# Moving tiles in the on-chip memory by 32 or 64 bytes, in a float32 transformer kernel

## The chip, the cores and the metric

The kernel runs on one core of a Trainium2 chip. The metric is the time of one launch in microseconds (us) of device time; lower is better. TensorE does the matrix products, VectorE (DVE) and ScalarE (ACT) the elementwise work, GpSimd (POOL) a little of it, and SyncE (SP) issues nearly all DMA transfers from device memory.

## What is computed

Two transformer blocks in float32 on 256 tokens of width 2048, batch 1. The first block is a pooling mixer layer (project 2048 to 2 x 4096, causal mean pools in four groups of 1024 channels, a 1024 x 1024 product in each group, a gate, project back) and a multi-head attention layer with latent keys and queries (16 heads, chunk-causal). The second block has a modulation vector `silu(c) @ w_mod` (2048 x 12288), an attention layer with 16 sliding-window heads and 16 top-k selected heads, and a gated feed-forward layer of inner width 5632 with a 3-tap convolution. Cut to what matters, all the heavy products have this form:

```python
h = rms_norm(x, norm_ffn) * (1.0 + sc2) + sh2
u, g = jnp.split(h @ w_up, 2, axis=-1)            # 2048 x 11264
u = conv3(u) + conv_b
x = x + g2 * ((jax.nn.silu(u) * g) @ w_down)      # 5632 x 2048
```

Each weight is used once, for all 256 tokens. About 480 MB are read, nearly all of it weights.

## The kernel before

**A slab.** All weights come as a stream of slabs, 128 partitions x 1024 float32 (4096 bytes in each partition), as a rule two k-tiles of 128 rows by 512 columns. A slab goes through a ring of four slots, `s = 0..3`. SP loads it into `raw[s]`. ACT copies it, rounded to the float32r type that TensorE takes at full rate, to `w_hi[s]` (line 611). DVE writes what the rounding left out, `raw - w_hi`, to `w_lo[s]` (line 1063). The activations are split in the same way into a high and a low tile of 1024 bytes per k-tile: `h_hi`/`h_lo`, `pool_hi`/`pool_lo`, `y_hi`/`y_lo`, `hk_hi`/`hk_lo`, `f_hi`/`f_lo` and a few more.

**A product.** `gemm` (the function around the line that the profile gives as L1690) takes for every slab 24 matrix instructions: for each of four column tiles of 128 weights and each of the two k-tiles, weights `w_hi` against the high and the low activations (16 instructions), then weights `w_lo` against the high activations (8). In each the 128 x 128 weight tile is the stationary operand (LDWEIGHTS, named PEld in the profile) and 256 tokens of the activation are the moving one (MATMUL). The weights of the next instruction are loaded while the present one streams. `acc<-h_hi,w_hi` in a row means: moving `h_hi`, stationary `w_hi`.

**Order.** TensorE's order is written out by hand; ACT and DVE count slabs (`split_to`) and put their other work between two splits. SP waits only for a slot to come free. Modulation tiles (`mod_raw`, `mod_acc`, line 1051) are worked off at due times between slabs. Outside `gemm` TensorE does the small attention products, column sums with a tile `ones`, and transposes.

**Homes.** Every tile has a fixed byte offset in its partition. `home(start, end)` hands out offsets one behind the other, rounded up to 32 bytes. The constants on line 121 give the regions: LOW (x, raw, tmp, tables), MOD_AT, W_AT (the eight weight slots), MID (tiles of a stage, reused from stage to stage), H_AT (h_hi, h_lo), FAR (further tiles of a stage) and the three modulation slots at the end. Slots and activation tiles are multiples of 1024 bytes long, so that every k-tile and every column tile of one buffer starts at the same residue of 128 bytes. Residues of the start offsets, worked out from these lines:

| tiles | offset before | mod 128 |
|---|---|---|
| raw0..3 | 32896 + 4096 s | 0 |
| w_hi0..3 | 82048 + 4096 s | 0 |
| w_lo0..3 | 98432 + 4096 s | 0 |
| h_hi, h_lo | 148288, 164672 | 64 |
| pool_hi/lo and hk_hi, y_hi/lo, f_hi/lo, c and q | 181056 and on | 64 |
| y_mid_hi, y_mid_lo (the y tiles of the third group) | 127616, 135808 | 0 |
| hk_lo | 114816 | 0 |
| mod_acc, prob | 73824, 220128 and on | 96 |
| m_prob, table | 139392, 57472 | 0 |

Of the kernel before, what the change touches and what calls it, by code (L numbers as in the profile page):

```python
# [16 lines left out]
F32R = mybir.dt.float32r  # L17
# [5 lines left out]
P = 128  # L23
TOK = 256
# [36 lines left out]
RING = 4  # L61
# [3 lines left out]
SLAB = SLAB_K * SLAB_N  # L65
# [52 lines left out]


SB_END = 229344  # L120
LOW, MOD_AT, W_AT, MID, H_AT, FAR = 16512, 73824, 82048, 114816, 148288, 181056
MOD_RING = 3
MOD_RAW_AT = SB_END - MOD_RING * 4096

# [56 lines left out]
def two_block_kernel(nc, t, out, cols):  # L181

    fixed = ExitStack()
    with fixed:
        def home(start, end):

            at = [start]

            def sb(name, shape, dt=F32):
                tile = nc.alloc_sbuf_tensor_at(name, shape, dt, offset=at[0])  # L190
                at[0] += -(-4 * int(np.prod(shape[1:])) // 32) * 32
                assert at[0] <= end, (name, at[0], end)
                return tile

            return sb
# [27 lines left out]
        warm = low("warm", [P, 1])  # L223

        mod_acc = home(MOD_AT, W_AT)("mod_acc", [P, D])
        ring = home(W_AT, MID)
        w_hi = [ring(f"w_hi{s}", [P, SLAB], F32R) for s in range(RING)]
        w_lo = [ring(f"w_lo{s}", [P, SLAB], F32R) for s in range(RING)]
        h_sb = home(H_AT, FAR)
        h_hi = h_sb("h_hi", [P, KD, TOK], F32R)  # L230
        h_lo = h_sb("h_lo", [P, KD, TOK], F32R)
# [25 lines left out]
        mid, far = home(MID, H_AT), home(FAR, MOD_RAW_AT - 1024)  # L257
        pool_hi = far("pool_hi", [P, 8, TOK], F32R)
        pool_lo = far("pool_lo", [P, 8, TOK], F32R)
        y_hi = far("y_hi", [P, 8, TOK], F32R)  # L260
        y_lo = far("y_lo", [P, 8, TOK], F32R)
        gate_a = mid("gate_a", [P, 8, TOK])
# [34 lines left out]
        far = home(FAR + 16384, MOD_RAW_AT - 1024)  # L297
# [12 lines left out]
        far = home(FAR, MOD_RAW_AT)  # L310
# [22 lines left out]
        mid, far = home(MID, H_AT), home(FAR, SB_END)  # L333
# [2 lines left out]
        f_raw = mid("f_raw", [P, 4, TOK])  # L336
        y_tok = [mid(f"y_tok{m}", [P, HALVES, 512]) for m in range(4)]
        x_gained = [conv, conv_silu, f_raw, mid("x_gained3", [P, 4, TOK])]
        f_hi = [far(f"f_hi{s}", [P, 4, TOK], F32R) for s in range(2)]
        f_lo = [far(f"f_lo{s}", [P, 4, TOK], F32R) for s in range(2)]  # L340


        raw_landed = [sem(f"raw_landed{s}") for s in range(RING)]
# [1857 lines left out]
```

How the kernel before makes its waits and increments, by code:

```python
            def load_mod():  # L407
                while mod_loads.total() < MOD_RING or mod_loads.total() < min(6 * MOD_TILES, MOD_RING + mod_due(slabs.total() - RING - 1)):
                    n = mod_loads.total()
                    v, j, slot = n // MOD_TILES, n % MOD_TILES, n % MOD_RING
                    if n >= MOD_RING:
                        sp.wait_ge(mod_used, n + 1 - MOD_RING)
                    sp.dma_start(mod_raw[slot][:, :], t["w_mod_2"][0][(j // 2) * P:(j // 2 + 1) * P, bass.ds(v * D + (j % 2) * 1024, 1024)])\
                        .then_inc(mod_landed[slot], 16)
                    mod_loads.step()
# [1 line left out]
            def load(src, k, n):  # L418
                sp.wait_ge(lo_ready, slabs.value(1))
                s = slabs.slot(RING)
                sp.dma_start(raw[s][:, 0:k * n].rearrange("p (k n) -> p k n", k=k),
                             src.rearrange("(k p) n -> p k n", p=P)).then_inc(raw_landed[s], 16)
                slabs.step()
                n = slabs.total()
                if n >= 2 * RING:
                    load_mod()
                if n == LINES_AT:
                    sp.wait_ge(line_ready, 1)
                    sp.dma_start(line_rows[:, :], lines[:, :]).then_inc(lines_out, 16)
                if 0 <= n - BIAS_STORE_AT < 2 * HEADS:
                    bias_store(n - BIAS_STORE_AT)
                if 0 <= n - BIAS_LOAD_AT < HEADS:
                    bias_load(0, n - BIAS_LOAD_AT)
```

## Time and profile before

| | |
|---|---|
| runs | 2190.24, 2191.16, 2227.77 us; median 2191.16 |
| span of the profiled execution | 2196.8 us |
| PE / PEld busy | 2107.0 (96%) / 2066.5 (94%) us |
| DVE / ACT busy | 1580.5 (72%) / 1007.4 (46%) us |
| DMA | 481.13 MB, 219 GB/s mean |
| granted TensorE clock, mean | 0.975 |

The span goes from the first to the last instruction of one profiled execution; no other time of that execution is given. The span stands 5.6 us above the median of the runs. A busy PE only says that some matrix instruction was in flight: they overlap, one is in flight for about 280 ns while a new one starts every 113 to 120 ns. The distance from start to start, the spacing, is what counts, and it is read from how many instructions fall in a window.

### The profile page before, as it was taken

How to read it: one execution, taken by the hardware profiler on the slowest of the kernel's cores; microseconds unless marked ns; L12 is line 12 of the kernel's file. 1: busy time of each engine (PE TensorE's matmuls, PEld its weight loads, DVE VectorE, ACT ScalarE, POOL GpSimd, SP SyncE). 2: the span in 40 equal slices, each digit the busy share in tenths (PEclk: the TensorE clock that was granted, in tenths of full speed). 3: DMA queues.
4: the chain of work that ended last, by engine and by line, in shares of the span. 5: the costliest groups of instructions: out<-in, count | busy, mean ns of one | idle time of the engine just before them, and what ended most of it. 6: DMA issues, size and time to landing. Idle time of an engine off the chain costs nothing.

```text
span 2196.8 us, 41578 instructions
## 1 busy us (share of the span) xinstructions
PE 2107.0 (96%) x17878; PEld 2066.5 (94%) x17878; DVE 1580.5 (72%) x2040; ACT 1007.4 (46%) x1285; POOL 42.1 (2%) x87
## 2 busy tenths in 40 slices
PE   7999999999999999999899778889999999999998
PEld 7999999999999999999899667789999999999997
DVE  7998796697687877787776567666666666666665
ACT  5443443444455665654444453544444444444443
POOL 1000000000000000000000110100000000000000
PEclk9999999999999999999999898999999999999998
DMA  7897887889575786668698244246666666666663
GB/s 241 275 338 270 299 299 255 270 293 326 197 244 170 243 267 227 201 238 314 210 339 269 50 123 147 87 135 191 198 196 193 193 193 193 190 202 192 193 194 103
DMA packets 248430, 481.13 MB, mean 219 GB/s; under 512 B 28331, under 2 KB 57623, under 8 KB 248247
## 3 DMA queue, kind: packets, MB, share of 16 engines
q1 hardware_dynamic: 247487, 478.26, 67.2%
q8 instruction: 141, 2.31, 0.4%
q14 instruction: 42, 0.34, 0.0%
q0 software_dynamic: 528, 0.15, 0.0%
q10 hardware_dynamic: 232, 0.06, 0.0%
HBM read 476.27 MB, written 8.44 MB: 221 GB/s over the span
## 4 chain that ended last, share of the span: by engine, by line
PE 86%; DVE 7%; issue 2%; DMA 2%; ACT 2%; POOL 0%; SPq 0%; DVEq 0%; ACTq 0%
PE acc L1690 81%; PE side L1690 2%; PE sums L1690 2%; DMA mod_raw<-in_w_mod 1%; DVE w_lo L1063 1%; DVE mod_acc L1051 1%; ACT w_hi L611 1%; POOL prob L591 0%; DMA vec_rows<-in_conv_b 0%; PE side L1919 0%; DVE prob L1523 0%; DVE prob L1521 0%; DVE a_max L1402 0%; DVE probT L1564 0%; PE sums L1919 0%
## 5 line engine op out<-in xcount | busy, mean ns | idle before, releaser
L1063 DVE TENSOR_TENSOR w_lo<-raw,w_hi 128x1024 fp32r<-128x1024 f32 x679 | 829.8, 1229 | 487.1 <-ACT w_hi L611 486.3
L611 ACT ACTIVATE w_hi<-raw 128x1024 fp32r<-128x1024 f32 x679 | 717.4, 1060 | 938.3 <-PE acc L1690 845.7
L1690 PE MATMUL acc<-h_hi,w_hi 128*128 128x256 f32 x3728 | 890.4, 280 | 17.4 <-issue 14.1
L1690 PE MATMUL acc<-h_lo,w_hi 128*128 128x256 f32 x3728 | 885.5, 279 | 0.0
L1690 PEld LDWEIGHTS acc<-h_hi,w_hi 128*128 128x128 f32 x3728 | 707.6, 190 | 23.8 <-issue 19.0
L1690 PEld LDWEIGHTS acc<-h_lo,w_hi 128*128 128x128 f32 x3728 | 708.2, 190 | 0.3 <-issue 0.2
L1690 PE MATMUL acc<-h_hi,w_lo 128*128 128x256 f32 x3728 | 507.1, 279 | 0.0
L1690 PEld LDWEIGHTS acc<-h_hi,w_lo 128*128 128x128 f32 x3728 | 465.3, 190 | 0.0
L1051 DVE SCALAR_TENSOR_TENSOR mod_acc<-mod_raw,silu_c,mod_acc 128x1024 f32<-128x1024 f32 x180 | 230.4, 1280 | 14.1 <-DMA mod_raw<-in_w_mod 13.9
L1690 PE MATMUL acc<-f_hi,w_hi 128*128 128x256 f32 x704 | 164.9, 277 | 4.0 <-DVE xT L1176 4.0
L1690 PE MATMUL acc<-f_lo,w_hi 128*128 128x256 f32 x704 | 164.8, 277 | 0.0
L1690 PEld LDWEIGHTS acc<-f_hi,w_hi 128*128 128x128 f32 x704 | 132.7, 189 | 4.2 <-DVE xT L1176 4.2
L1690 PEld LDWEIGHTS acc<-f_lo,w_hi 128*128 128x128 f32 x704 | 132.8, 189 | 0.0
L1690 PE MATMUL acc<-f_hi,w_lo 128*128 128x256 f32 x704 | 94.8, 277 | 0.0
L1690 PE MATMUL acc<-y_hi,w_hi 128*128 128x256 f32 x384 | 94.4, 285 | 0.0
L1690 PE MATMUL acc<-y_lo,w_hi 128*128 128x256 f32 x384 | 92.0, 279 | 0.0
L1176 DVE SCALAR_TENSOR_TENSOR xT<-acc,mod,xT 128x256 f32<-128x256 f32 x208 | 86.0, 476 | 4.6 <-PE acc L1690 4.6
L1690 PEld LDWEIGHTS acc<-f_hi,w_lo 128*128 128x128 f32 x704 | 87.2, 189 | 0.0
L1690 PEld LDWEIGHTS acc<-y_hi,w_hi 128*128 128x128 f32 x384 | 73.4, 191 | 0.2 <-DVE tmp L1206 0.2
L1690 PEld LDWEIGHTS acc<-y_lo,w_hi 128*128 128x128 f32 x384 | 73.2, 191 | 0.0
L1690 PE MATMUL acc<-pool_hi,w_hi 128*128 128x256 f32 x256 | 59.6, 276 | 0.0
L1690 PE MATMUL acc<-pool_lo,w_hi 128*128 128x256 f32 x256 | 59.6, 276 | 0.0
(312 smaller groups left out, 2048.5 us busy)
## 6 DMA issues: line engine op xcount, KB each, us to landing
mod_raw<-in_w_mod SPq DMA_DIRECT2D x192, 512.0 KB, 6.0
raw<-in_w_up SPq DMA_DIRECT2D x176, 512.0 KB, 4.4
raw<-in_a_w_in SPq DMA_DIRECT2D x128, 512.0 KB, 5.1
raw<-in_w_down SPq DMA_DIRECT2D x88, 512.0 KB, 4.3
raw<-in_a_w_out SPq DMA_DIRECT2D x64, 512.0 KB, 4.7
raw<-in_w_in SPq DMA_DIRECT2D x56, 512.0 KB, 4.3
raw<-in_b_w_in SPq DMA_DIRECT2D x40, 512.0 KB, 4.6
raw<-in_a_w_group SPq DMA_DIRECT2D x32, 512.0 KB, 5.4
```

The costliest lines, as they stand in the source:

```text
L611: last = act.activation(w_hi[s][:, :], raw[s][:, :], ACT.Copy)
L1051: ins = dve.scalar_tensor_tensor(o, x[:, :], silu_c[:, j // 2:j // 2 + 1], o, ALU.mult, ALU.add)
L1063: last = dve.tensor_tensor(w_lo[s][:, :], raw[s][:, :], f32(w_hi[s][:, :]), ALU.subtract)
L1176: last = dve.scalar_tensor_tensor(x, acc[s][:, n, :], mod[:, scale, bass.ds(m + n, 1)], x, ALU.mult, ALU.add)
L1690: return pe.matmul(o, lhsT, rhs, start=start, stop=stop, skip_group_check=True)
```

## The change

The offsets of tiles change and nothing else: no instruction, no order, no wait, no size.

```diff
-LOW, MOD_AT, W_AT, MID, H_AT, FAR = 16512, 73824, 82048, 114816, 148288, 181056
+LOW, MOD_AT, W_AT, MID, H_AT, FAR = 16512, 73824, 82048, 115136, 148288, 181088
...
-        ring = home(W_AT, MID)
-        w_hi = [ring(f"w_hi{s}", [P, SLAB], F32R) for s in range(RING)]
-        w_lo = [ring(f"w_lo{s}", [P, SLAB], F32R) for s in range(RING)]
+        w_hi = [home(W_AT + 4128 * s, MID)(f"w_hi{s}", [P, SLAB], F32R) for s in range(RING)]
+        w_lo = [home(W_AT + 16512 + 4128 * s, MID)(f"w_lo{s}", [P, SLAB], F32R) for s in range(RING)]
...
         pool_lo = far("pool_lo", [P, 8, TOK], F32R)
+        far = home(FAR + 16384 + 64, MOD_RAW_AT - 1024)
         y_hi = far("y_hi", [P, 8, TOK], F32R)
         y_lo = far("y_lo", [P, 8, TOK], F32R)
...
-        f_hi = [far(f"f_hi{s}", [P, 4, TOK], F32R) for s in range(2)]
-        f_lo = [far(f"f_lo{s}", [P, 4, TOK], F32R) for s in range(2)]
+        f_sb = [home(FAR + 8256 * s, SB_END) for s in range(2)]
+        f_hi = [f_sb[s](f"f_hi{s}", [P, 4, TOK], F32R) for s in range(2)]
+        f_lo = [f_sb[s](f"f_lo{s}", [P, 4, TOK], F32R) for s in range(2)]
```

The residues of 128 bytes that follow: w_hi and w_lo of slot s at 32 s (0, 32, 64, 96); h_hi and h_lo at 64, as before; pool, hk_hi, c and q at 96; y_hi and y_lo at 32; f_hi and f_lo at 96 (buffer 0) and 32 (buffer 1); everything in MID, y_mid and hk_lo with it, at 64. The raw slots, x, tmp and the modulation tiles stay.

## Rows read from the trace of the kernel before

**Rows 1.** The page: busy time of the engines, and two rows of the span's 40 slices.
```profile
PE 2107.0 (96%) x17878; PEld 2066.5 (94%) x17878; DVE 1580.5 (72%) x2040; ACT 1007.4 (46%) x1285; POOL 42.1 (2%) x87
...
PEclk9999999999999999999999898999999999999998
```
**Rows 2.** The chain that ended last, by engine, and its longest pieces (start, us, what).
```profile
PE 86%; DVE 7%; issue 2%; DMA 2%; ACT 2%; POOL 0%; SPq 0%; DVEq 0%; ACTq 0%
...
1454.90 709.67 PE acc L1690 x6240
```
**Rows 3.** The page, costliest groups: the two splits of a slab.
```profile
L1063 DVE TENSOR_TENSOR w_lo<-raw,w_hi 128x1024 fp32r<-128x1024 f32 x679 | 829.8, 1229 | 487.1 <-ACT w_hi L611 486.3
L611 ACT ACTIVATE w_hi<-raw 128x1024 fp32r<-128x1024 f32 x679 | 717.4, 1060 | 938.3 <-PE acc L1690 845.7
```
**Rows 4.** Windows: length, busy us (count) of PE, PEld, DVE, ACT, POOL; clock; DMA.
```profile
40.00:140.00 100.00, 100.00 (x884) 100.00 (x884) 87.92 (x105) 44.87 (x45) 0.00 (x0) 1.00 0.85 285
580.00:600.00 20.00, 20.00 (x169) 20.00 (x168) 11.99 (x12) 7.43 (x7) 0.00 (x0) 1.00 0.68 227
620.00:640.00 20.00, 20.00 (x179) 20.00 (x178) 15.08 (x20) 12.05 (x14) 2.40 (x1) 1.00 0.73 247
1600.00:2100.00 500.00, 500.00 (x4414) 500.00 (x4413) 325.40 (x412) 209.24 (x199) 0.00 (x0) 1.00 0.65 195
```
**Rows 5.** Windows of the slower stretches of products with h, and one with c.
```profile
684.00:691.00 7.00, 7.00 (x62) 7.00 (x61) 2.70 (x4) 5.27 (x9) 0.00 (x0) 1.00 0.29 78
967.00:983.00 16.00, 16.00 (x139) 16.00 (x138) 12.84 (x19) 7.24 (x14) 0.00 (x0) 1.00 0.76 251
991.00:1001.00 10.00, 10.00 (x87) 10.00 (x86) 6.12 (x7) 7.08 (x8) 0.00 (x0) 1.00 0.60 199
1067.00:1200.00 133.00, 133.00 (x1131) 133.00 (x1130) 100.80 (x96) 57.10 (x59) 0.00 (x0) 1.00 0.86 296
1308.00:1352.00 44.00, 44.00 (x376) 44.00 (x375) 35.04 (x68) 17.75 (x17) 0.00 (x0) 1.00 0.60 188
749.00:753.00 4.00, 4.00 (x36) 4.00 (x35) 3.39 (x8) 3.97 (x6) 0.00 (x0) 1.00 1.05 369
```
**Rows 6.** Groups by line, 1460 to 2160 us, products with h and f.
```profile
L1690 PE MATMUL acc<-h_hi,w_hi 128*128 128x256 f32 x1400 | 326.0, 276 | 0.0
L1690 PEld LDWEIGHTS acc<-h_lo,w_hi 128*128 128x128 f32 x1400 | 262.9, 188 | 0.0
```
**Rows 7.** Groups by line, 1080 to 1180 us, products with h.
```profile
L1690 PE MATMUL acc<-h_hi,w_hi 128*128 128x256 f32 x283 | 68.3, 281 | 0.0
```
**Rows 8.** Groups by line, 575 to 608 us, products with y_mid; then 612 to 640 us, with y.
```profile
L1690 PE MATMUL acc<-y_mid_hi,w_hi 128*128 128x256 f32 x95 | 23.3, 283 | 0.0
...
L1690 PE MATMUL acc<-y_hi,w_hi 128*128 128x256 f32 x84 | 19.6, 276 | 0.0
```
**Rows 9.** Groups by line, 655 to 676 us, products with hk.
```profile
L1690 PE MATMUL acc<-hk_lo,w_hi 128*128 128x256 f32 x56 | 13.5, 280 | 0.0
L1690 PE MATMUL acc<-hk_hi,w_hi 128*128 128x256 f32 x56 | 13.4, 279 | 0.0
L1690 PE MATMUL acc<-hk_hi,w_lo 128*128 128x256 f32 x62 | 8.4, 277 | 0.0
```
**Rows 10.** Timeline of PE (start, length of a merged piece), one slab of hk.
```profile
657.14 0.28 PE L1690 MATMUL acc<-hk_hi,w_hi 128*128 128x256 f32 x1
657.26 0.28 PE L1690 MATMUL acc<-hk_lo,w_hi 128*128 128x256 f32 x1
657.38 0.51 PE L1690 MATMUL acc<-hk_hi,w_lo 128*128 128x256 f32 x3
```
**Rows 11.** Timeline of PE, 885.4 to 888.2 us: sums with mod_acc, small attention products.
```profile
885.96 0.72 PE L1690 MATMUL side<-ones,mod_acc 128*128 128x1 f32 x6
...
887.55 0.82 PE L1919 MATMUL sums<-table,m_prob 128*128 128x128 f32 x6
```
**Rows 12.** Timeline of PEld, the same stretch.
```profile
885.84 0.75 PEld L1690 LDWEIGHTS side<-ones,mod_acc 128*128 128x128 f32 x6
```
**Rows 13.** Timeline of PE, 1256 to 1262 us: a small product with prob.
```profile
1255.74 0.71 PE L1919 MATMUL side<-table,prob 128*128 128x128 f32 x5
```

## The prediction, made before the changed kernel ran

> **What bounds the kernel now.** Read the page first: TensorE has an instruction in flight for 96% of the span and its clock stands near full almost throughout [rows 1]. The chain of waits says the same in another way: 86% of it is TensorE, and its longest piece is a single run of 709.67 us with 6240 products and not one wait [rows 2]. So the time is a number of matrix instructions times their spacing. The two splits are hidden: for each slab ACT works 1060 ns and DVE 1229 ns, one behind the other 2.29 us, while TensorE needs 24 x 113.3 ns = 2.72 us, and ACT stood idle 938 us, nearly all of it waiting for TensorE to free a slot [rows 3]. A split that gets some nanoseconds longer or shorter moves nothing. That leaves one question: does the spacing depend on where the operands lie?
>
> The window view answers it in part. About 2.4 instructions are in flight at a window's edge, so a count less 2.4 gives the spacing. In the feed-forward layer it is 500 us / 4411.6 = 113.3 ns, and at the start of the kernel the same, 100 / 881.6 = 113.4 [rows 4]. DMA busy share and DVE load differ there (0.85 against 0.65, 88% against 65%), the spacing doesn't, so neither of them sets it. But the third pooling group, whose moving operand is y_mid, runs at 20 / 166.6 = 120.0 ns, and 20 us later the fourth group with y_hi at 20 / 176.6 = 113.3, both at clock 1.00 [rows 4]. The two are the same code, the same shapes and the same weight slots. A single product is in flight 283 ns against 276 [rows 8], the same 276 as in the feed-forward layer [rows 6]; it is 7 ns longer, just what the spacing grew. What differs is the home: y_mid lies at residue 0 of 128 bytes, as the weight slots do, and y at 64. The kv stage is a second witness. There hk_hi (64) and hk_lo (0) take turns, and the products take 279 and 280 ns, halfway; under w_lo, where hk_hi stands alone, 277 on average [rows 9].
>
> There is a third spacing. In five stretches with h, whose residues are the same as in the fast stretches, it is 117.8 ns (133 us / 1128.6 in the longest), and 281 ns in flight [rows 5, 7]. Clock is 1.00 there. So for one pair of homes there are two rhythms, and TensorE stays in the one in which it falls after a pause, for over a thousand instructions. I read all three as the weight load and the moving stream getting into each other's way at the memory; in which way, no row tells.
>
> **Taken literally, a rule speaks against the change having any effect.** The Trainium skill, SBUF — State Buffer, section Who interferes with whom, gives TensorE two independent read ports and says that PE and ACT "never wait on anyone". By it the kernel would take 2191 after the change. The y_mid row (120.0 against 113.3 ns) does not agree; that the kernel's other spacings depend on homes is not shown.
>
> **The terms.** No instruction is added or removed, so every term is a count times a difference of spacings.
>
> 1. Slow rhythm. The stretches of [rows 5] hold 62 + 139 + 87 + 1131 + 376 = 1795 instructions, less five times 2.4 = 1783; the stretch with c comes once for each of eight head pairs with some 34, 270 in all. 2050 x (117.8 - 113.3 = 4.45 ns) = 9.1 us. A weight slot now keeps its residue for one slab only, so a rhythm that lives on one relation of the two streams should not survive the next slab. I take the whole 9.1 us as a gain. Bounds: nothing, and a loss if the slow rhythm spreads (a rival).
> 2. y_mid, 384 products, moves from residue 0 to 64: 384 x 6.67 ns = 2.6 us. hk: 80 products each of three kinds, 5, 4 and 2 ns over 276 on the page's averages with [rows 9], 0.9 us.
> 3. Change of relation at each slab. Leaving the alternating pattern of hk, three products took 0.51 us, (0.51 - 0.28) / 2 = 117 ns of spacing, before 113 came back [rows 10]: some 3 x 3.5 = 10 ns. About 700 slabs x 10 ns = 7 us lost. From both sides: nothing, if the rhythm is kept, and 24 x 4.45 ns x 700 = 75 us, if it is never regained.
> 4. Residues 32 and 96. No float32r product of before has them, so they are bounded: below by the row of the weight loads alone, above by 120.0. Six weight loads for one-column products last 0.75 us, (0.75 - 0.19) / 5 = 112 ns apart [rows 12], and six small products of 128 columns in plain float32 0.82 us, (0.82 - 0.27) / 5 = 110 [rows 11]. A spacing under 112 therefore isn't to be had, and 113.3 is already near the floor. I take 113.3, because a 32-byte offset alone does no harm: mod_acc, the stationary operand of [rows 12], lies at residue 96, and prob, a moving one, too, and its five products last 0.71 us, (0.71 - 0.27) / 4 = 110 ns [rows 13], as m_prob at residue 0 [rows 11].
> 5. ACT and DVE: w_lo and w_hi change place against raw. Between 0 and some 10 ns each, hidden by the 0.43 us for each slab worked out above; without that cover 700 x 10 ns = 7 us. The pieces at the two attention stages, where TensorE waits for them, are few.
>
> Sum: -9.1 - 2.6 - 0.9 + 7 = -5.6 us. The profiled span (2196.8) stands 5.6 us above the median of the runs, 0.3%, and its own time outside the span isn't given; the difference is carried to the median: 2191.2 - 5.6 = 2185.6, say 2186.
>
> **Rivals.** A ruler for them: 679 full slabs x 24 = 16,300 products, so 1 ns of mean spacing is 16.3 us. The mean now is 113.33 + (9.1 + 2.6 + 0.9) / 16.3 = 114.1 ns.
>
> *A. A quarter of the slabs collides (slower).* If 120 ns belongs to equal residues, the change brings the collision to every stage. h is at 64 and slot 2 now too; pool meets slot 3 (96), y slot 1 (32), f slots 3 and 1. Exactly one slab in four then runs like y_mid: 4075 x 6.67 = 27.2 us, against the gains 2191 - 12.6 + 27.2 = 2206, with term 3 2213. It decides from a mean spacing above 114.1. If residues 32 apart are half as bad, another 8150 x 3.33 = 27.2 us come on top, 2233 to 2240. For it: y_mid and hk. Against: two examples don't say whether the period is 128 bytes or 256 or 512 (modulo 512, y_mid minus weights is 0 and h minus weights 192); with a period of 512 only the w_lo products of one slot collide with h, 1 in 12, +9 us, which is 2188 to 2194.
>
> *B. The slow rhythm spreads (slower).* If each new relation throws TensorE into 117.8 ns and it stays there: 13,900 x 4.45 = 62 us, less 3: 2250; at 120 everywhere 2289. Against: after hk the fast rhythm came back within half a slab.
>
> *C. Homes don't matter here.* 120 and 117.8 come from how a stage starts, and y_mid is chance. 2191; if the 6240 products of the feed-forward run draw the slow rhythm, 27.8 us more, 2219. For it: h with unchanged homes shows both rhythms. Against: y_mid kept 120 through some 290 products and lost it at once with y.
>
> *D. The streams part better than before (faster).* With residues 32 apart the spacing drops to the weight-load floor of about 111.7: 2191 - 12.6 - 16.3 x 1.6 = 2152. At the 109.2 ns of the small products it would be 2111, but their weight loads are shorter than ours. [...]
>
> **Chances.** Forecast (2178 to 2193) 0.36; A 0.20 for the quarter alone, 0.09 with the half-bad neighbours; B 0.09; C 0.16; D 0.10. Two per cent, about what a measurement here can tell from no change, is 2147 and 2235. Faster than that is only the far part of D, 0.05. Slower is B and some half of the worse A, with a little for a pattern not thought of: 0.15. Within: 0.80. The range of 2151 to 2236 takes in the forecast, C, both bounds of A's quarter, most of D, and leaves B, the rest of A and the far part of D out. The forecast's own range is 2178 to 2193.
>
> **What would show it.** Term 1: a window at 1067 to 1200 us holds about 1176 instructions, not 1131. Term 2: y_mid products 276 ns in flight, not 283. Terms 3 and 4: 500 us of the feed-forward layer hold at least 4390; A shows as one slab in four at 283 ns and about 4350 in that window; B as 4250. DVE and ACT: the splits within 10 ns of 1229 and 1060, and ACT still waiting for TensorE. The prediction is wrong if the feed-forward window leaves 4390 to 4430, or if the time moves while those counts don't.

## The result and the profile after

The changed kernel takes 2245.8 us in the median of four runs (2243.41 to 2248.74). The kernel before, run four times beside it, took 2205.53 in the median; the ratio is 1.0224, 95% interval 1.016 to 1.0287. Ratios here and below leave out runs more than 1.5% above the fastest of the same kernel. It is slower, by about two per cent (the lower end of the interval is 1.6%), where 2186 was forecast with a range of 2151 to 2236.

The kernel before scatters more than the changed one: of 19 later runs on one chip 14 took 2187 to 2200 us and 5 took 2219 to 2234 (median 2196.64), and of 11 more runs there two lay between, at 2205 and 2215. The profiled executions are 2242.3 us long after and 2196.8 before, 45.5 us apart.

Engines and clock of the changed kernel, from its page. They answer to [rows 1]: the same number of instructions, the same mean clock (0.977 against 0.975), TensorE 51 us longer busy.

```profile
PE 2158.2 (96%) x17878; PEld 2118.9 (94%) x17878; DVE 1583.4 (71%) x2040; ACT 1008.3 (45%) x1285; POOL 42.1 (2%) x87
```

The two splits of a slab, from the same page, against [rows 3].

```profile
L1064 DVE TENSOR_TENSOR w_lo<-raw,w_hi 128x1024 fp32r<-128x1024 f32 x679 | 830.0, 1230 | 530.7 <-ACT w_hi L612 528.2
L612 ACT ACTIVATE w_hi<-raw 128x1024 fp32r<-128x1024 f32 x679 | 718.0, 1061 | 987.2 <-PE acc L1691 938.4
```

They last what they lasted, within 1 ns, and ACT waits longer for TensorE (938.4 us, not 845.7). Three pieces of the chain of waits (start, us, what), against [rows 2], and two windows, against [rows 4]:

```profile
21.51 183.16 PE acc L1691 x1540
...
1083.20 137.92 PE acc L1691 x1156
...
1475.42 735.09 PE acc L1691 x6240
```

```profile
40.00:140.00 100.00, 100.00 (x855) 100.00 (x854) 85.30 (x99) 43.15 (x43) 0.00 (x0) 1.00 0.82 278
1600.00:2100.00 500.00, 500.00 (x4260) 500.00 (x4259) 315.76 (x400) 202.34 (x193) 0.00 (x0) 1.00 0.59 187
```

Here the time is. The same 6240 products of the feed-forward layer take 735.09 us, not 709.67: 25.4 us. The 500 us window holds 4260 instructions, not 4414, a spacing of 500 / 4257.6 = 117.4 ns. The clock is 1.00 in both windows. The layer also starts later, at 1475.42 us and not at 1454.90, which is another 20.5 us; the two together are 45.9, and the rest of the kernel gives 0.4 of it back. Part of the 20.5 us is seen in the first long piece. It is this piece before:

```profile
21.34 176.97 PE acc L1690 x1540
```

It takes 6.2 us longer now, 4.0 ns for each product, and the window at the start says the same: 100 / 852.6 = 117.3 ns against 113.4.

One level deeper, the timeline of TensorE shows the eight w_lo products of five slabs in a row as merged pieces (start, length), and the first w_hi product of a slab by itself.

```profile
1685.24 1.07 PE L1691 MATMUL acc<-h_hi,w_lo 128*128 128x256 f32 x8
1686.15 0.28 PE L1691 MATMUL acc<-h_hi,w_hi 128*128 128x256 f32 x1
...
1688.03 1.10 PE L1691 MATMUL acc<-h_hi,w_lo 128*128 128x256 f32 x8
1688.96 0.28 PE L1691 MATMUL acc<-h_hi,w_hi 128*128 128x256 f32 x1
...
1690.86 1.12 PE L1691 MATMUL acc<-h_hi,w_lo 128*128 128x256 f32 x8
1691.82 0.28 PE L1691 MATMUL acc<-h_hi,w_hi 128*128 128x256 f32 x1
...
1693.74 1.10 PE L1691 MATMUL acc<-h_hi,w_lo 128*128 128x256 f32 x8
1694.68 0.28 PE L1691 MATMUL acc<-h_hi,w_hi 128*128 128x256 f32 x1
...
1696.51 1.07 PE L1691 MATMUL acc<-h_hi,w_lo 128*128 128x256 f32 x8
```

The length less the 0.28 us that the last product is in flight, over seven, is the spacing under w_lo: 113, 117, 120, 117, 113 ns. From the first w_hi product of a slab to its first w_lo product there are 16 spacings: 1.88, 1.90, 1.92 and 1.83 us, or 117.5, 118.8, 120.0 and 114.4 ns. The pattern repeats after four slabs, the length of the ring. Whether this is the stagger of the slots, and what in it, is for the experiments.

### The profile page after: what moved, and what is told of

It is laid out like the page before. It is cut to its first block, busy times and chain, and to the rows that moved or that the text cites. A ratio compares the mean times of both kernels' runs of the same rounds, so it can differ in the third digit from the quotient of the medians.

```text
span 2242.3 us, 41578 instructions
## 1 busy us (share of the span) xinstructions
PE 2158.2 (96%) x17878; PEld 2118.9 (94%) x17878; DVE 1583.4 (71%) x2040; ACT 1008.3 (45%) x1285; POOL 42.1 (2%) x87
## 4 chain that ended last, share of the span: by engine, by line
PE 89%; DVE 6%; DMA 2%; issue 2%; ACT 1%; POOL 0%; SPq 0%; DVEq 0%; ACTq 0%
PE acc L1691 84%; PE side L1691 3%; PE sums L1691 2%; DVE w_lo L1064 1%; DMA mod_raw<-in_w_mod 1%; DVE mod_acc L1052 1%; ACT w_hi L612 1%; POOL prob L592 0%; PE side L1920 0%; DMA vec_rows<-in_conv_b 0%; DVE prob L1522 0%; DVE a_max L1403 0%; DVE prob L1524 0%; DVE probT L1565 0%; PE sums L1920 0%
## 5 line engine op out<-in xcount | busy, mean ns | idle before, releaser
L1064 DVE TENSOR_TENSOR w_lo<-raw,w_hi 128x1024 fp32r<-128x1024 f32 x679 | 830.0, 1230 | 530.7 <-ACT w_hi L612 528.2
L612 ACT ACTIVATE w_hi<-raw 128x1024 fp32r<-128x1024 f32 x679 | 718.0, 1061 | 987.2 <-PE acc L1691 938.4
L1691 PE MATMUL acc<-h_hi,w_hi 128*128 128x256 f32 x3728 | 916.0, 284 | 14.9 <-issue 12.0
L1691 PE MATMUL acc<-h_lo,w_hi 128*128 128x256 f32 x3728 | 910.5, 283 | 0.0
L1691 PE MATMUL acc<-h_hi,w_lo 128*128 128x256 f32 x3728 | 518.4, 282 | 0.0
L1691 PEld LDWEIGHTS acc<-h_hi,w_lo 128*128 128x128 f32 x3728 | 476.5, 191 | 0.0
L1691 PE MATMUL acc<-f_hi,w_hi 128*128 128x256 f32 x704 | 170.3, 282 | 4.0 <-DVE xT L1177 4.0
L1691 PE MATMUL acc<-f_lo,w_hi 128*128 128x256 f32 x704 | 169.8, 281 | 0.0
```

What stands on the lines that cost most here:

```text
L612: last = act.activation(w_hi[s][:, :], raw[s][:, :], ACT.Copy)
L1064: last = dve.tensor_tensor(w_lo[s][:, :], raw[s][:, :], f32(w_hi[s][:, :]), ALU.subtract)
L1691: return pe.matmul(o, lhsT, rhs, start=start, stop=stop, skip_group_check=True)
```

## The experiments

Theory R, nearest to the prediction's rival A: the spacing depends on the offset between the start of the moving and the start of the stationary tile, taken as a remainder of some power of two. Its rivals are U, that a start which is no multiple of 64 bytes makes a tile slow by itself; H, that homes don't matter and the spacing is drawn when a stage starts; and S, that the stagger is harmless and the moved regions cost the time. In all that follows "offset" is moving minus stationary start. In the kernel before it was 192 as a remainder of 512 for h, pool, y, hk_hi, f, c and q, and 0 for y_mid and hk_lo.

**Weights back in line, regions still moved (e1).**

```diff
-        w_hi = [home(W_AT + 4128 * s, MID)(f"w_hi{s}", [P, SLAB], F32R) for s in range(RING)]
-        w_lo = [home(W_AT + 16512 + 4128 * s, MID)(f"w_lo{s}", [P, SLAB], F32R) for s in range(RING)]
+        ring = home(W_AT, MID)
+        w_hi = [ring(f"w_hi{s}", [P, SLAB], F32R) for s in range(RING)]
+        w_lo = [ring(f"w_lo{s}", [P, SLAB], F32R) for s in range(RING)]
```

> The changed kernel with its weight slots back in line (all eight at residue 0 of 128 bytes, 4096 apart); the middle and far regions, y and f stay moved. Theory R (what counts is the offset of the moving tile against the stationary one): the products with h regain one steady spacing, 113.3 or 117.8 ns, those with y_mid and hk_lo (now 64 off) too, while f, pool and y (32 or 96 off) stay at an in-between value of 115 to 118; a window of 100 us with only h in the feed-forward layer holds 849 to 885 instructions. Total 2195 to 2225 us. Theory S (the stagger does nothing, the moved regions alone cost the time): about 2245 as the changed kernel. Theory U (a tile whose start is 32 past a multiple of 64 streams slowly): only pool, y, f, hk_hi, c and q slow, h at 113.3 or 117.8, so this run can't tell R from U except by h.

2211.85 us (10 runs), ratio to before 1.0068 (1.0037 to 1.0099). Three windows of it: products with h at the start of the kernel, a pooling group's products with pool, whose offset is 224, and the feed-forward layer.

```profile
40.00:100.00 60.00, 60.00 (x512) 60.00 (x511) 49.55 (x61) 25.09 (x24) 0.00 (x0) 1.00 0.73 233
...
274.00:294.00 20.00, 20.00 (x171) 20.00 (x170) 16.67 (x17) 9.19 (x9) 0.00 (x0) 1.00 0.88 300
...
1600.00:2100.00 500.00, 500.00 (x4358) 500.00 (x4357) 325.24 (x413) 208.25 (x198) 0.00 (x0) 1.00 0.64 191
```

The tile pool runs at 20 / 168.6 = 118.6 ns where it had 113.3. The feed-forward window holds 4358, between 4414 and 4260, for h is at 113.3 again there and f isn't. So with the weights in line a loss of 0.7% is left, not nothing and not all: S falls. Not even the 0.7% is all due to the moved regions: in this trace h, at its old offset of 192, ran at 60 / 509.6 = 117.7 ns at the start of the kernel, the slow rhythm that the kernel before shows in other stages.

**The stagger alone (e2)**, the second half of the diff above put into the kernel before, with MID at 115200 to make room.

> The kernel before with the staggered weight slots alone (residues 0, 32, 64, 96 of 128); h, pool, y, f at 64 as before; the middle region is moved by 384 bytes to make room, which keeps its residue 0. Theory R: every stage with moving tiles at 64 shows four kinds of slabs, slot 0 near 114 to 115 ns, slot 2 near 119 to 120, slots 1 and 3 117 to 120, as the changed kernel's h slabs did; mean about 117.5; total about 2245, the whole loss. Theory S: about 2191. Theory U: slots 1 and 3 slow, slots 0 and 2 both at 113.3.

2246.57 us, ratio 1.0215 (1.0156 to 1.0274): the whole loss. The feed-forward window holds 4263, and the w_lo pieces go round as in the changed kernel:

```profile
1686.12 1.12 PE L1689 MATMUL acc<-h_hi,w_lo 128*128 128x256 f32 x8
1689.00 1.10 PE L1689 MATMUL acc<-h_hi,w_lo 128*128 128x256 f32 x8
1691.77 1.07 PE L1689 MATMUL acc<-h_hi,w_lo 128*128 128x256 f32 x8
1694.55 1.10 PE L1689 MATMUL acc<-h_hi,w_lo 128*128 128x256 f32 x8
```

U wanted two kinds of slab and gets three. On top of the stagger the moved regions cost nothing more, since no tile has a steady offset left to lose.

**Roles swapped (e3).** Weights 64 bytes on, the middle region 128.

```diff
-LOW, MOD_AT, W_AT, MID, H_AT, FAR = 16512, 73824, 82048, 114816, 148288, 181056
+LOW, MOD_AT, W_AT, MID, H_AT, FAR = 16512, 73824, 82048, 114944, 148288, 181056
...
-        ring = home(W_AT, MID)
+        ring = home(W_AT + 64, MID)
```

> The kernel before with all eight weight slots moved by 64 bytes together (residue 64), and the middle region by 128 (residue 0). Now h, pool, y, f, c and q lie 0 off the weights and y_mid and hk_lo 64 off. Theory R: the roles swap: 120.0 ns for h, pool, y and f (283 ns in flight, a feed-forward window of 500 us holds 4169), 113.3 or 117.8 for y_mid; total about 2280 to 2290. Theory H (homes don't matter, the rhythm is drawn when a stage starts) and theory U: 2191 to 2220 and y_mid as before or as any other.

2270.43 us, ratio 1.0325 (1.0263 to 1.0386). Two windows:

```profile
40.00:100.00 60.00, 60.00 (x508) 60.00 (x507) 49.76 (x61) 25.11 (x24) 0.00 (x0) 1.00 0.73 232
...
1600.00:2100.00 500.00, 500.00 (x4169) 500.00 (x4168) 310.79 (x397) 197.99 (x188) 0.00 (x0) 1.00 0.62 183
```

Every start of these tiles is a multiple of 64 here, and the feed-forward layer runs at the predicted 4169, 120.0 ns. U and H fall: with every start a multiple of 64 all the layer is slow, and it is slow by its homes. But at the start of the kernel it is 60 / 505.6 = 118.7, so offset 128 isn't quite offset 0, and the total stays 10 us under what was expected.

**All tiles of the products 32 bytes on (e4).** Weights, MID, H_AT and FAR all +32, offsets as before; the raw and modulation slots stay.

> The kernel before with the weight slots, the middle region, h and the far region all moved by 32 bytes together: every offset of a moving against a stationary weight tile is as before, but all of them start 32 past a multiple of 64. Theory R: as before, 113.3 ns in most stages, 120.0 for y_mid, 117.8 in some, 2185 to 2230 in all. Theory U: every product slow, 117 or more, 2240 or more.

2206.14 us (10 runs, 2192.7 to 2236.96), ratio 1.0014 (0.9973 to 1.0054). y_mid at 169 instructions in 20 us and the feed-forward layer at 4414, to the instruction what [rows 4] show:

```profile
580.00:600.00 20.00, 20.00 (x169) 20.00 (x168) 13.64 (x13) 7.45 (x7) 0.00 (x0) 1.00 0.69 233
1600.00:2100.00 500.00, 500.00 (x4414) 500.00 (x4413) 325.43 (x412) 209.52 (x200) 0.00 (x0) 1.00 0.65 194
```

A start 32 past a multiple of 64 costs nothing by itself in these windows. Seven of its ten runs took 2193 to 2211 us and three 2226 to 2237, one of them above the 2230 expected.

**Which remainder counts (e5 to e8).** Slots in line, one offset for all products; the edit is e3's, with other numbers: W_AT + 128 and MID 115008 (offset 64), W_AT + 256 and MID 115520 (448), W_AT + 384 and MID 115520 (320), W_AT + 192 and MID 115008 (0).

> Offset of moving against stationary tile, as a remainder of 512 bytes, has been 192 for h, pool, y and f in the kernel before. Here the eight weight slots (in line) move by 128 bytes and the middle region by 192, so that every product, y_mid and hk_lo too, has the offset 64. If only the remainder of 128 counts: 113.3 ns as a rule and 117.8 in some stretches, no 120.0 anywhere, 2180 to 2230. If the remainder of 256 or 512 counts: another spacing than 113.3 in the feed-forward layer; y_mid at 64 in the swapped kernel ran at 117.8, so 117.8 throughout and about 2250 would be the other answer.

> As the run with offset 64, but the weight slots move by 256 bytes and the middle region by 704: offset 448 of 512 (which is 192 of 256, as before) for every product. If the remainder of 256 counts and not that of 512: as before, 113.3 ns in the feed-forward layer with 117.8 in some stretches, 2180 to 2230. If 512 counts, something else.

> As the run with offset 64, with the weight slots moved by 384 and the middle region by 704: offset 320 of 512 (64 of 256, 64 of 128) for every product. y_mid at 320 in the kernel with the weights back in line ran at 117.8 in all of its 384 products. Either that was drawn, and this kernel is at 113.3 in most stages (2180 to 2230), or 320 belongs to 117.8 (about 2250).

> All eight weight slots (in line) and the middle region move by 192 bytes, so that every moving tile lies 0 off the weight tiles as a remainder of 512, as y_mid did before. The relation theory: 120.0 ns in every stage, 283 ns in flight, a window of 500 us in the feed-forward layer holds 4169, total 2275 to 2295. In the swapped kernel the offset was 128 of 512 and the spacing 118.7 to 120.0; if 0 and 128 are the same to the chip, this one varies in the same way.

One run each: 2244.33, 2191.8, 2252.51 and 2281.97 us, and 2198.29 for the kernel before beside them. The feed-forward windows, of e5 (offset 64), e6 (448), e7 (320) and e8 (0):

```profile
1600.00:2100.00 500.00, 500.00 (x4248) 500.00 (x4247) 315.58 (x399) 202.20 (x192) 0.00 (x0) 1.00 0.63 186
```
```profile
1600.00:2100.00 500.00, 500.00 (x4414) 500.00 (x4413) 325.45 (x412) 209.45 (x199) 0.00 (x0) 1.00 0.65 194
```
```profile
1600.00:2100.00 500.00, 500.00 (x4248) 500.00 (x4247) 313.45 (x397) 201.10 (x191) 0.00 (x0) 1.00 0.63 187
```
```profile
1600.00:2100.00 500.00, 500.00 (x4169) 500.00 (x4169) 311.00 (x396) 197.51 (x188) 0.00 (x0) 1.00 0.62 183
```

Spacings 117.8, 113.3, 117.8 and 120.0. 448 behaves as 192 and 320 as 64, so a period of 256 bytes fits what was seen. A period of 128 would make 64 and 192 the same, and since both offsets show both rhythms, one window doesn't decide; the count over all traces speaks for 256. In the feed-forward layer all six traces with offset 192 for every tile of that layer (before, e4, e6, e10, e11, e12) hold 4414 or 4415, and both with 64 hold 4248. At 40 to 140 us the six hold 884 or 885 and the two 852; e1's h at 192, slow there, is the one exception. Offset 0 gives 120 ns at the start of e8 as well, 60 / 499.6 = 120.1, where offset 128 gave 118.7:

```profile
40.00:100.00 60.00, 60.00 (x502) 60.00 (x502) 48.98 (x60) 24.76 (x24) 0.00 (x0) 1.00 0.71 229
```

That is the y_mid of before, now with h. Offset 64 gives the slow rhythm, but not by necessity: in e5 one stage of products with h fell into the fast one and a later one into the slow one.

```profile
1326.00:1366.00 40.00, 40.00 (x355) 40.00 (x354) 33.79 (x67) 16.96 (x17) 0.00 (x0) 1.00 0.61 191
1420.00:1460.00 40.00, 40.00 (x342) 40.00 (x342) 24.58 (x29) 18.01 (x17) 0.00 (x0) 1.00 0.60 178
```

**The remaining offsets (e9).** Weights in line; h at 160, pool, f, hk_hi, c and q at 96, y at 32, y_mid at 0.

```diff
-LOW, MOD_AT, W_AT, MID, H_AT, FAR = 16512, 73824, 82048, 114816, 148288, 181056
+LOW, MOD_AT, W_AT, MID, H_AT, FAR = 16512, 73824, 82048, 114816, 148256, 181216
...
+        far = home(197792, MOD_RAW_AT - 1024)
         y_hi = far("y_hi", [P, 8, TOK], F32R)
```

> The kernel before with its weights in line and the moving tiles at offsets not yet seen in a steady stage: h at 160 of 256 bytes, pool, hk_hi, c, q and f at 96, y at 32, y_mid and hk_lo at 0 as before. By the period of 256 found so far (192 fast, 64 slow rhythm, 0 at 120.0, 128 at 118.7 to 120.0), these lie between: 116 to 119.5 each, nothing under 113.3, total 2240 to 2275. If an offset exists at which the streams part better than at 192, one of them shows less than 113.3 ns.

2273.1 us in one run. Windows with h, with pool, with y_mid and with y:

```profile
40.00:100.00 60.00, 60.00 (x508) 60.00 (x507) 49.88 (x62) 25.11 (x24) 0.00 (x0) 1.00 0.74 235
278.00:298.00 20.00, 20.00 (x169) 20.00 (x168) 16.43 (x17) 9.02 (x9) 0.00 (x0) 1.00 0.87 291
590.00:620.00 30.00, 30.00 (x253) 30.00 (x252) 19.02 (x19) 10.62 (x10) 0.00 (x0) 1.00 0.65 208
640.00:670.00 30.00, 30.00 (x257) 30.00 (x256) 24.36 (x31) 17.66 (x20) 4.81 (x2) 1.00 0.63 198
```

118.7 ns at 160, 120.0 at 96, 119.7 at 0, 117.8 at 32. The weight slots and the raw slots lie where they lay in the kernel before; only the moving tiles have moved. None of the eight offsets seen beats 113.3; 96 is a little worse than was expected. One instruction more or less in a window of 20 us is 0.7 ns, so 117.8, 118.6 and 118.7 are hardly apart. The table as the runs give it, at clock 1.00:

| offset mod 256 | spacing, ns | from |
|---|---|---|
| 0 | 120.0 | y_mid before, e8 |
| 32 | 117.8 | y of e9 |
| 64 | 117.8, at times 113.3 | e5, e7 |
| 96 | 120.0 | pool of e9 |
| 128 | 118.7 or 120.0 | e3 |
| 160 | 118.7 | h of e9 |
| 192 | 113.3, at times 117.8 | before, e6 |
| 224 | 118.6 | pool of e1 |

The changed kernel can be worked out from it. Its h lies at 192, 160, 128 and 96 under w_hi of slots 0 to 3 and at 64, 32, 0 and 224 under w_lo. By the table, with 118.7 for 128 and 113.3 for 64, that is 113.3, 118.7, 118.7, 120.0 and 113.3, 117.8, 120.0, 118.6 ns. The timeline of the changed kernel has 114.4, 117.5, 118.8, 120.0 and 113, 117, 120, 117. Which slab lies in which slot isn't in the trace; the order alone fits. The mean by the table, 16 products of the first kind to 8 of the second, is 117.6 ns; measured were 117.4.

**Raw slots staggered (e10)**, the same 32-byte steps for tiles that TensorE never reads.

```diff
-        raw = [low(f"raw{s}", [P, SLAB]) for s in range(RING)]
+        raw = [home(LOW + 16384 + 4128 * s, MOD_AT)(f"raw{s}", [P, SLAB]) for s in range(RING)]
+        low = home(LOW + 16384 + 4 * 4128, MOD_AT)
```

> The kernel before with the four raw slots staggered by 32 bytes in place of the weight slots (tmp and the tables behind them move by 128); TensorE never reads raw, ACT, DVE and the DMA do. If the stagger costs time because two streams of TensorE meet: no effect, 113.3 ns in the feed-forward layer, 2187 to 2234 as the kernel before draws it, ACT's split 1060 ns and DVE's 1229 within 10 ns. If it were the writes and reads of ACT, DVE or DMA against each other: TensorE's spacing or the splits change, 2240.

2193.64 us in one run, 4414 in the feed-forward window, splits at 1060 and 1229 ns. A stagger of the raw slots, which changes where ACT, DVE and the DMA read and write, is not the cause; and in e9 neither raw nor weight slots moved, while the spacing did.

**The kernel before once more (e11), and the best candidate timed (e12, the same as e6).**

> The kernel before, unchanged, one more traced execution. Its runs so far fall in two groups, 2187 to 2200 and 2219 to 2234 us. If the groups are which rhythm the long run of the feed-forward layer draws (6240 instructions x 4.45 ns = 27.8 us), an execution of 2219 us or more shows 117.8 ns there and one under 2200 shows 113.3; the stages with h before it differ from those of the first trace by chance too.

> The kernel with offset 448 of 512 (192 of 256) for every product, y_mid and hk_lo too, timed. Against the kernel before, y_mid gains 384 x 6.7 ns = 2.6 us and hk about 1; the draw of the slow rhythm stays. 0.997 to 1.0 of the kernel before. If more: the slow rhythm is drawn less often with it.

e11 took 2196.27 us, under the 2200 of the expectation, and shows 113.3 ns in the feed-forward layer, as expected of such a run. The window of 1080 to 1180 us, however, held 851 in the first trace of this very kernel (first line) and holds 885 in e11 (second):

```profile
1080.00:1180.00 100.00, 100.00 (x851) 100.00 (x850) 77.11 (x64) 41.75 (x41) 0.00 (x0) 1.00 0.96 336
...
1080.00:1180.00 100.00, 100.00 (x885) 100.00 (x884) 79.64 (x67) 43.24 (x43) 0.00 (x0) 1.00 0.97 342
```

So the rhythm of a stage is drawn anew in each execution. e6 and e12 are one kernel too, and the window of 1000 to 1040 us holds 355 in the one and 342 in the other:

```profile
1000.00:1040.00 40.00, 40.00 (x355) 40.00 (x355) 33.48 (x29) 16.27 (x16) 0.00 (x0) 1.00 0.96 341
```
```profile
1000.00:1040.00 40.00, 40.00 (x342) 40.00 (x341) 32.91 (x29) 16.64 (x16) 0.00 (x0) 1.00 0.95 342
```

e12 took 2193.99 us (6 runs), ratio to before 1.0013 (0.9962 to 1.0065). y_mid now holds 179 instructions in 20 us, as y does, which is the 2.6 us that were wanted; the draw of a stage (27.8 us for the feed-forward layer alone) hides it. The kernel of e12 beats the changed kernel and can't be told from the kernel before. No execution of before above 2200 us was caught in a trace. That in those of 2219 us and more the feed-forward layer has the slow rhythm rests on the distance alone, 6240 x 4.45 ns = 27.8 us from 2192 to 2220, and stays open.

## Why the prediction was wrong

The reading of what bounds the kernel held: only the spacing changed, TensorE still had 96% of the span, and splits and clock stood. The idea of rival A, that equal or unequal homes of the two operands decide, held as well, with another period. The forecast did not follow it. The prediction's own sign, 4390 to 4430 instructions in the feed-forward window, came out at 4260.

**Term 4 is the step that failed.** It took 113.3 ns for the residues 32 and 96, "because a 32-byte offset alone does no harm". That sentence is true (e4), and has no bearing: what counts is not the residue of a tile but its offset against the other stream. The rows called in are of another kind. The sums with mod_acc have a moving operand of one column, the small products with prob one of 128 columns and a weight load of 140 ns where the heavy products have 188; a 256-column operand never streams there. By the notation of the rows prob is moreover the stationary operand, not the moving one. They gave a floor for the spacing and were read as its value. Measured, 32, 96, 160 and 224 give 117.8, 120.0, 118.7 and 118.6. Term 4 was put at nothing; in the feed-forward layer alone it cost 25.4 us. By the prediction's ruler the mean spacing rose from 114.1 to 117.4 ns, 3.3 x 16.3 = 54 us for the float32r products, of which 45.5 show in the span. The ruler also counts products in stages where TensorE waits for other engines or its clock is lower; that these hide the missing 8 us isn't shown.

**Term 1**, 9.1 us gained from the slow rhythm, came to nothing. The stagger did break the rhythm, as was argued, but into the mean of four offsets, 137.92 us for the piece of 1156 products against 138.44 before. And the slow rhythm is drawn anew in each execution (e11), so a gain read off one trace was a draw as well.

**Term 2**: y_mid went from 283 ns in flight to 281 and 280, 20 / 169.6 = 117.9 ns of spacing in its window, a gain of 0.8 us, not 2.6. It left one bad offset for eight, of which 0 is again one. The hk products, from which 0.9 us were to come, went from 279, 280 and 277 ns in flight to 281, 280 and 280: no gain. e6 gives y_mid its 2.6.

**Term 3** holds where it can be seen. Its sum has a slip: (0.51 - 0.28) / 2 is 115 ns, not 117, which halves the 10 ns for each slab. In most slabs of the changed kernel there is no fast rhythm to come back to. In the slab of the timeline at 1694.68 us there is one, and its 16 spacings take 1.83 us, about 17 ns more than 16 x 113.3, where the timeline is good to 10 ns.

**Term 5** was right: 1230 and 1061 ns, hidden.

**The rivals.** A with half-bad neighbours, chance 0.09, had the mechanism and nearly the size: 2233 to 2240 against 2245.8. It was short because the neighbours are not half-bad but two thirds to wholly so. The full collision, offset 0, is met by one product with h in twelve and not by one in four. Its doubt about the period was justified: a period of 256 fits the runs and 128 doesn't, so each slot brings two offsets, one for w_hi and one for w_lo. B was wrong as put (no spread of the slow rhythm), though an offset of 64 for all slots gives just that, and about its price (2244 to 2253 for a forecast of 2250). (At 120 everywhere its sum gives 2287, not 2289.) C is refuted by e3 and e8, but its half about the draw is right. D was not seen: nothing under 113.3 at any of eight offsets. Its far bound of 2111 stood on 109.2 ns, which no run shows; the rows give 110 for the small products, and these have 128 columns, not 256. The rule quoted from the Trainium skill, SBUF — State Buffer, section Who interferes with whom, would have had e8 at the time of the kernel before, 2198 us beside it; it took 2282, with no instruction of any engine changed. The measurement decides: with both operands read as before in all but their addresses, TensorE starts its products 5.9% further apart. What in the chip makes it so, no run shows.

The range should have reached 2250, by its own table: B and A's worse half stood at 0.18 together, while the forecast had 0.36 with its weakest term, the fourth, backed by no row of a float32r product.

## What to carry to other kernels

When one pair of operands is slower than another of the same shape, compare the start addresses of the two streams that run at the same time, not each address by itself, and keep one good offset for all buffers in place of a stagger. The stagger here averaged over eight offsets, the bad ones included. And if the times of a kernel scatter by more than its change is worth, count instructions in a window of each stage over several traces before reading a few microseconds from one.

## What the runs showed of the hardware

float32r products of 128 x 128 weights and 256 columns, weights loaded anew for each, start 113.3 to 120.0 ns apart at full clock, by the offset of moving against stationary start as a remainder of 256 bytes (the table above): 5.9% between best and worst, 2282 us (e8, one run) against 2192 (e6, one run) for this kernel. At offsets 192 and 64 there are two stable rhythms, 113.3 and 117.8 ns; the long stages kept one all through, up to the 6240 products of the feed-forward layer, and the same kernel draws differently from execution to execution (851 and 885 instructions in the same 100 us). Moving both operands of all heavy products by 32 bytes together changes nothing that can be told (1.0014, 0.9973 to 1.0054).
